# Gathered expert rows replaced by a dense sweep over all experts, once for each pair of token blocks

## The reference, cut to what matters

```python
def peer_ffn(h, w_q, sub_keys, u, v):          # u, v: (16384, 1024) a layer, 64 MB each
    def block(xb):                              # xb: 128 tokens x 1024
        q = (xb @ w_q).reshape(BLK, PEER_HEADS, PEER_QDIM)
        s1 = einsum('thd,hkd->thk', q[..., :64], sub_keys[:, 0])
        s2 = einsum('thd,hkd->thk', q[..., 64:], sub_keys[:, 1])
        v1, i1 = top_k(s1, 16); v2, i2 = top_k(s2, 16)
        cand = (v1[..., :, None] + v2[..., None, :]).reshape(BLK, 8, 256)
        sc, ci = top_k(cand, 16)
        e = i1[ci // 16] * 128 + i2[ci % 16]    # 8 heads x 16 = 128 experts a token
        g = softmax(sc)
        a = gelu(einsum('thkd,td->thk', u[e], xb)) * g
        return einsum('thk,thkd->td', a, v[e])
```

## Time and profile before

| | |
|---|---|
| runs | 2941.36 us median of 3 (2940.45 to 2948.73) |
| profiled execution, span from first to last instruction | 2939.0 us |
| PE, DVE, ACT, POOL busy | 78%, 74%, 40%, 44% |
| bytes read from HBM | 1164.28 MB, 398 GB/s with those written |

### The profile page before, as it was taken

How to read it: one execution, slowest core, us unless ns; L and a number is a source line. 1 busy time by engine, 2 the same in 40 slices (tenths; PEclk the granted TensorE clock), 3 DMA queues, 4 the chain that set the end, 5 groups by cost and what they waited for, 6 DMA issues and landing times.

```text
span 2939.0 us, 27902 instructions
## 1 busy us (share of the span) xinstructions
PE 2279.9 (78%) x7308; PEld 1206.3 (41%) x7308; DVE 2186.8 (74%) x5158; ACT 1182.4 (40%) x3443; POOL 1282.0 (44%) x1186
## 2 busy tenths in 40 slices
PE   8578787687887887787787878877788777886767
PEld 6535453354433544243443435433443434432222
DVE  2497768775878757796688877978779786887664
ACT  2144434343443433344444453435534454433333
POOL 0144334443355433454434544345434454355555
PEclk9789989999898998998899998989889898998889
DMA  6499999999999999999999999999999999999998
GB/s 253 150 401 421 404 362 422 420 421 389 413 410 421 421 393 412 421 411 421 414 382 402 421 421 416 392 403 417 421 406 392 405 421 421 391 411 422 422 422 359
DMA packets 170941, 1170.16 MB, mean 398 GB/s; under 512 B 19681, under 2 KB 19937, under 8 KB 36401
## 3 DMA queue, kind: packets, MB, share of 16 engines
q0 software_dynamic: 147456, 1073.81, 88.7%
q1 hardware_dynamic: 23344, 94.74, 8.2%
HBM read 1164.28 MB, written 4.19 MB: 398 GB/s over the span
## 4 chain that ended last, share of the span: by engine, by line
DMA 25%; DVE 15%; PE 12%; issue 6%; ACT 4%; POOL 3%; POOLq 0%; DVEq 0%; ACTq 0%; SPq 0%
DMA ring<-in_uv,pick_now 23%; PE acc L1650 7%; DVE ring L1076 5%; POOL ring L662 3%; PE ps L1448 3%; DVE side L1069 1%; DMA xc<-h 1%; ACT diag L1343 1%; DMA stream<-in_strips 1%; DVE arena L955 1%; ACT coef L1333 1%; DVE arena L936 1%; DVE arena L1026 1%; DVE arena L1030 1%; DVE arena L937 1%
## 5 line engine op out<-in xcount | busy, mean ns | idle before, releaser
L1650 PE MATMUL acc<-ring,diag 128*128 128x512 f32 x2988 | 1554.2, 663 | 487.9 <-ACT diag L1343 486.7
L662 POOL DMA_INDIRECT ring<-in_uv,pick_now x1024 | 1225.1, 1196 | 1514.3 <-PE acc L1650 1046.9
L1076 DVE CUSTOM_DVE_ANT_0 ring<-ring,h_now 128x1024 f32<-128x1024 f32 x1024 | 1237.3, 1223 | 518.5 <-DMA ring<-in_uv,pick_now 506.8
L1650 PEld LDWEIGHTS acc<-ring,diag 128*128 128x128 f32 x2988 | 586.3, 208 | 1316.9 <-ACT diag L1343 743.2
L1330 ACT ACTIVATE gelu<-dots 128x1 f32<-128x1 f32 x1024 | 206.1, 201 | 1253.9 <-DVE dots L1076 1252.4
L1069 DVE SCALAR_TENSOR_TENSOR side<-ring,coef,side 128x1024 f32<-128x1024 f32 x270 | 346.0, 1282 | 32.1 <-ACT coef L1333 32.0
L1343 ACT ACTIVATE diag<-ident,coef 128x128 f32<-128x128 f32 x747 | 300.0, 402 | 68.8 <-PE acc L1650 44.7
L1333 ACT ACTIVATE coef<-gate,gelu 128x1 f32<-128x1 f32 x1024 | 301.5, 294 | 33.2
L1448 PE MATMUL ps<-resident,actT 128*128 128x256 f32 x896 | 219.5, 402 | 0.0
L1448 PEld LDWEIGHTS ps<-resident,actT 128*128 128x128 f32 x896 | 177.1, 201 | 44.2 <-issue 19.6
L1435 PE MATMUL ps<-actT,stream 128*128 128x128 f32 x992 | 131.0, 294 | 28.5 <-DMA stream<-in_strips 24.3
(11 more groups left out here) (193 smaller groups left out, 1429.5 us busy)
## 6 DMA issues: line engine op xcount, KB each, us to landing
stream<-in_strips SPq DMA_DIRECT2D x104, 512.0 KB, 8.2
resident<-in_strips SPq DMA_DIRECT2D x18, 1024.0 KB, 12.4
ring<-in_uv,pick_now POOLq DMA_INDIRECT x1024, 12.5
ring<-in_strips SPq DMA_DIRECT2D x8, 1024.0 KB, 19.6
arena<-in_keys SPq DMA_DIRECT2D x8, 512.0 KB, 7.7
xc<-in_x SPq DMA_DIRECT2D x4, 512.0 KB, 6.9
h<-arena SPq DMA_DIRECT2D x4, 512.0 KB, 11.2
xc<-h SPq DMA_DIRECT2D x4, 512.0 KB, 7.8
```

The costliest lines, as they stand in the source:

```text
L662: pool.indirect_dma_start(ring[:, i, :], None, tables[layer], bass.IndirectOffsetOnAxis(ap=pick_now[:, half, i:i + 1], axis=0),).then_inc( ...
L1076: dve.tensor_tensor_reduce(ring[:, i, 0:D], ring[:, i, 0:D], h_now[:], 1.0, 0.0, ALU.mult, ALU.add, dots[:, i:i + 1]).then_inc(dotted, 1)
L1650: m = pe.matmul(acc[:, b * 512:(b + 1) * 512], diag[:, i % 4, :], ring[:, i, D + b * 512:D + (b + 1) * 512], start=(r == 0 and i == tensor ...
```

## The change

The eight stages become four passes of two blocks each: blocks (0, 1) and (2, 3) of layer 0, then of layer 1. A pass reads the whole `u` and the whole `v` of its layer, with plain DMAs from SP, and has three phases, counted in beats (`BEATS`):

- 128 beats "u": a tile of 128 experts is turned on DVE by two 32 x 32 block transposes (`turn_u`), and PE makes its dots with all tokens of the pass, eight products of 256 columns (`dot`). After every second tile ACT writes the gelu of them into `coef`, 128 tiles x 256 tokens (`gelu`).
- 64 beats "group" of four tokens: for each token DVE makes two matrices of 128 x 128 from `iota` (one-hot of one half of the expert's number; one-hot of the other half times the gate, `mark_lists`), PE multiplies them (`place`), which gives the token's gates over all 16384 experts, ACT copies the four out of the accumulator (`take_lists`), and POOL multiplies them into `coef`.
- 128 beats "v": a beat is 256 experts x 512 columns of `v`, and PE adds four products of 512 columns (`sum_up`), after a product with the identity that puts the residual ("seed") in.

Weight strips (none is kept now), `u`, seeds and `v` all go through one ring of four units of 512 KB. A new `AT` gives the beat before which each piece of the mixers and choices stands, for each block. In pass 0 the mixers of blocks 0 and 1 both stand before the first beat, their two choices beside the u phase; the mixer of block 2 begins at beat 128 and goes on beside the v phase, the mixer of block 3 has its last pieces at beats 318 to 320. In all passes nearly no piece stands between beats 132 and 192 of the pass. The gain of the second norm is now applied by ACT as a scale, and POOL copies the turned block to `hT2` (`keep`). The values of all tensors stay float32.

```diff
-SLOTS = 8
-RESIDENT = 9
+RING = 4
+TURNS = 3
+QUADS = 4
+TOKENS = 4
+PASSES = ((0, (0, 1)), (0, (2, 3)), (1, (0, 1)), (1, (2, 3)))
+def beats():
+    for n in range(len(PASSES)):
+        yield from (("u", n, i) for i in range(TILES))
+        yield from (("group", n, i) for i in range(groups_in(n)))
+        yield from (("v", n, i) for i in range(TILES))
...
@@ sync
+                elif u.what == "u":
+                    n, tile = u.key
+                    if tile % 2 == 0:
...
+                        for q in range(QUADS):
+                            sp.dma_start(
+                                ring[q * 32:(q + 1) * 32, at:at + 2, :].rearrange("p s (g c) -> p (s g) c", g=QUADS),
+                                tables[PASSES[n][0]][tile * P:(tile + 2) * P, q * STRIP:(q + 1) * STRIP].rearrange(
+                                    "(g j) c -> j g c", j=32),
+                            ).then_inc(loaded[at], 16)
@@ gpsimd
-                            pool.indirect_dma_start(
-                                ring[:, i, :], None, tables[layer],
-                                bass.IndirectOffsetOnAxis(ap=pick_now[:, half, i:i + 1], axis=0),
-                            ).then_inc(got[i], 16)
+                for group in range(groups_in(n)):
+                    at = groups_before(n) + group
+                    pool.wait_ge(built, at + 1)
+                    c = coef[:, :, group * TOKENS:(group + 1) * TOKENS]
+                    pool.tensor_tensor(c, c, lists[:, group % TURNS], ALU.mult).then_inc(scaled, 1)
@@ vector
-                        dve.tensor_tensor_reduce(ring[:, i, 0:D], ring[:, i, 0:D], h_now[:], 1.0, 0.0, ALU.mult,
-                                                 ALU.add, dots[:, i:i + 1]).then_inc(dotted, 1)
+            def mark_lists(n, group):
...
+                for i in range(TOKENS):
+                    t = group * TOKENS + i
+                    at = groups_before(n) * TOKENS + t
+                    if at >= TOKENS:
+                        dve.wait_ge(placed, at - TOKENS + 1)
+                    inner, outer = work[:, 2 * i * P:(2 * i + 1) * P], work[:, (2 * i + 1) * P:(2 * i + 2) * P]
+                    dve.tensor_scalar(inner, iota[:], listT[:, 2, t:t + 1], None, ALU.is_equal)
+                    dve.tensor_scalar(outer, iota[:], listT[:, 1, t:t + 1], listT[:, 0, t:t + 1], ALU.is_equal,
+                                      ALU.mult).then_inc(hot, 1)
+            def turn_u(n, tile):
...
+                for c in range(CUTS):
+                    m = 2 * (n * TILES + tile) + c
...
+                        dve.wait_ge((turn_used, dotted)[(m - TURNS) % 2], (m - TURNS) // 2 + 1)
+                    dve.transpose(turned_u[:, m % TURNS].rearrange("p k (g j) -> p g k j", g=QUADS),
+                                  u[:, :, c * CUT:(c + 1) * CUT, :]).then_inc(turned, 1)
@@ scalar
-                        act.activation(diag[:, i % 4, :], ident[:], ACT.Copy,
-                                       scale=coef[:, i:i + 1]).then_inc(diag_ready, 1)
+            def take_lists(n, group):
...
+                if group >= TURNS:
+                    act.wait_ge(scaled, at - TURNS + 1)
+                act.activation(lists[:, group % TURNS],
+                               acc[:, group % 2 * 512:(group % 2 + 1) * 512].rearrange("p (t i) -> p i t", t=TOKENS),
+                               ACT.Copy).then_inc(built, 1)
@@ tensor
-                            m = pe.matmul(acc[:, b * 512:(b + 1) * 512], diag[:, i % 4, :],
-                                          ring[:, i, D + b * 512:D + (b + 1) * 512],
-                                          start=(r == 0 and i == tensor[0][0]), stop=True, skip_group_check=True)
+            def dot(n, tile):
...
+                dst = acc[:, tile % 4 * 2 * P:(tile % 4 + 1) * 2 * P][:, tokens_of(n)]
+                for c in range(CUTS):
+                    m = 2 * at + c
+                    pe.wait_ge(turned, m + 1)
+                    for k in range(CUT):
+                        i = pe.matmul(dst, turned_u[:, m % TURNS, k, :], hT2[:, c * CUT + k, tokens_of(n)],
+                                      start=(c == 0 and k == 0), stop=(c == CUTS - 1 and k == CUT - 1))
+                    i.then_inc((turn_used, dotted)[c], 1)
+            def place(n, group):
...
+                if group >= 2:
+                    pe.wait_ge(built, at - 1)
+                for i in range(TOKENS):
+                    pe.wait_ge(hot, TOKENS * at + i + 1)
+                    pe.matmul(acc[:, (group % 2 * TOKENS + i) * P:(group % 2 * TOKENS + i + 1) * P],
+                              work[:, 2 * i * P:(2 * i + 1) * P], work[:, (2 * i + 1) * P:(2 * i + 2) * P],
+                              start=True, stop=True).then_inc(placed, 1)
+            def sum_up(n, v):
...
+                w = unit("v", n, v).rearrange("p (t c) -> p t c", t=2)
+                for t in range(2):
+                    for slot in range(2):
+                        i = pe.matmul(acc[:, slot * HALF_D:(slot + 1) * HALF_D],
+                                      coef[:, 2 * j + t, slot * P:(slot + 1) * P], w[:, t, :], start=False, stop=True,
+                                      skip_group_check=True)
+                i.then_inc(swept, 1)
```

More of the change, by code:

```diff
@@ L1 @@
 from contextlib import ExitStack
-from itertools import chain
 import numpy as np
@@ L69 @@
[L69 to L86, removed]
-    "gla": {
[13 rows of a table removed]
+CUT = KT // CUTS
+TILES = EXPERTS // P
+HALF_D = D // 2
+RING = 4
+TURNS = 3
+QUADS = 4
+TOKENS = 4
+SAYS = (
+    {1: "q", 3: "k", 7: "v", 11: "r", 15: "y", 16: "pq0", 17: "pq1", 18: "pq2", 19: "pq3"},
+    {3: "q", 4: "kv", 8: "y", 9: "pq0", 10: "pq1", 11: "pq2", 12: "pq3"},
+)
@@ new lines, in said, with chosen, preps_of, chain @@
+    def said(self, engine, event):
+        names = EVENTS[self.kind][engine]
+        base = BLOCKS * len(EVENTS["gla"][engine]) if self.layer else 0
+        return self.p * len(names) + base + names.index(event) + 1
+    def chosen(self, engine, event):
+        names = CHOSEN[engine]
+        return self.turn * len(names) + names.index(event) + 1
+def preps_of(n):
+    return [Prep(n, slot) for slot in range(len(PASSES[n][1]))]
+def chain():
+    for n in range(len(PASSES)):
+        preps = preps_of(n)
+        if n == 0:
+            yield from ((prep.kind, prep) for prep in preps)
+            yield from (("pick", prep) for prep in preps)
+        else:
+            for prep in preps:
+                yield prep.kind, prep
+                yield "pick", prep
@@ new lines, with blocks_in, groups_in, groups_before @@
+CHAIN = list(chain())
+def blocks_in(n):
+    return len(PASSES[n][1])
+def groups_in(n):
+    return blocks_in(n) * P // TOKENS
+def groups_before(n):
+    return sum(groups_in(m) for m in range(n))
+def sweep(n):
+    if blocks_in(n) == 2:
+        return [(h, j) for h in range(2) for j in range(TILES // 2)]
+    return [(h, j) for j in range(TILES // 2) for h in range(2)]
+def begins(n, v):
+    return v % (TILES // 2 if blocks_in(n) == 2 else TILES) == 0
+def phases_before(n):
+    return sum(blocks_in(m) for m in range(n))
@@ new lines, in stores_before, with beats_in, order @@
+def stores_before(n):
+    return sum((4 if blocks_in(m) == 2 else 1) for m in range(n))
+def beats_in(n):
+    return groups_in(n) + 2 * TILES
+def beats():
+    for n in range(len(PASSES)):
+        yield from (("u", n, i) for i in range(TILES))
+        yield from (("group", n, i) for i in range(groups_in(n)))
+        yield from (("v", n, i) for i in range(TILES))
+BEATS = list(beats())
+def order(engine):
+    return sorted((beat, i, piece) for i, (kind, prep) in enumerate(CHAIN)
+                  for piece, beat in zip(PIECES[kind][engine], AT[i][engine]))
@@ L239, in __call__, with beside @@
         self.settle()
+def beside(engine, pieces, dense):
+    at = [next(p) for p in pieces]
+    done = 0
+    for beat, i, piece in order(engine):
+        while done < int(beat):
+            dense(*BEATS[done])
+            done += 1
+        assert at[i] == piece, (engine, at[i], piece)
+        at[i] = next(pieces[i], None)
+    for beat in BEATS[done:]:
+        dense(*beat)
 def build(nc, x, positions, gain_mix, gain_ffn, strips0, strips1, w_lr, w_alpha, b_alpha, gla_gain,
@@ new lines, in choose @@
+                for half in range(2):
+                    each = onehot[:, half, 0:H * TOPK * TOPK].rearrange("p (h k j) -> p h k j", h=H, j=TOPK)
+                    step.mark(dve.tensor_tensor(
+                        each, each, both(topf)[:, half, hs].rearrange("p h (o j) -> p h o j", o=1).to_broadcast(
+                            [P, H, TOPK, TOPK]), ALU.mult))
+                step.settle()
+                dve.tensor_reduce(ef[:, :, hs].rearrange("p a h k -> p a (h k)"), hits, AX, ALU.add)\
+                   .then_inc(chosen["dve"], 1)
@@ new lines, in dense @@
+            def dense(what, n, beat):
+                if what == "u":
```

(20 more changed lines are left out.)

1526 lines of the change are left out of this document (733 added, 793 removed), and 55 rows, old and new, of tables (AT, LATE, PIECES, STRIPS_OF).

## The result

The changed kernel takes 5125.22 us (median of 4 runs, 5123.13 to 5129.81); the kernel before took 2942.43 (2940.45 to 2948.73, 4 runs beside it). The ratio is 1.7425, 95% interval 1.7399 to 1.7451: much slower, as forecast (5200), and 75 us under the forecast.

What follows compares the result with a forecast made beforehand. Bytes (DMA) were taken to bound the kernel before, DVE and PE each at three quarters. Terms 1782 + 1771 + 540 + 210 + 768 + 57 + 60 + 8 = 5196 us, forecast 5200, range 4800 to 5650.

Steps and rivals of the forecast that it cites:

- A: PE's dots in the u phases: 4096 products of 256 columns at 0.435 us, 1782 us.
- B: PE's sums in the v phases: 2048 products of 512 columns and 16 seeds at 0.858 us, 1771 us.
- C: PE's other work outside the opening, taken from its earlier busy time: 540 us.
- D: Opening: mixers 0 and 1 one after the other ahead of the first dot, 210 us with POOL's copy.
- E: Group phases: 256 groups, DVE's 2.0 us and POOL's 1.0 one after the other, 768 us.
- F + G + H: In order: seams between phases 57 us, PE's pieces with late DVE or ACT partners 60, the last store 8.
- Rival 3: PE's pieces wait (5390 us), or its clock is 0.91 throughout, dots and sums rising by 351 (5550); chance 0.14.
- Rival 1: Group phases: DVE and POOL run beside each other, POOL's 1.0 us hidden behind 2.0, time 4944 us; chance 0.2.
- rival 2: Group phases: POOL's product or the tokens' chain is slow, 4.2 us a group, time 5500 us; chance 0.12.
- The load, put at nothing: u phase: loading 1 MB takes 3.5 us and hides behind PE's 7.0, with two pairs in the ring.
- Rival 4: The u load sets the pace, deciding from about 10 us a MB; at 12.4, +1380 us, time 6580; chance 0.07.
- Rival 5: Whole kernel: not slower, the halved bytes decide at 1.7 ms because PE's dense products cost less; chance 0.01.

Runs made afterwards that it cites:

- consts_first: The changed kernel with POOL making its constants before, not after, it issues its 16 small loads: 5124.31 us.
- pool_quarter: The changed kernel with three quarters of POOL's multiplication in the group phases left out: 4911.14 us.
- dve_mul: The changed kernel with the group's product moved from POOL to DVE, which reads the gates straight from the accumulator: 4993.23 us.
- half_k: The changed kernel with half of each dot's products left out, all loads kept: 4740.35 us.
- half_k_spread: As half_k, but each DMA of u writes a quarter of the columns to all 128 partitions instead of all columns to 32: 4586.3 us.
- quarter: The changed kernel with three of four chunk products of each half dot and three quarters of each sum's columns left out: 3958.23 us.

## Why the prediction came out right, step by step

| term | forecast | measured | from |
|---|---|---|---|
| A dots | 1782 | 1794 | L1667 |
| B sums and seeds | 1771 | 1797 | L1702 1774.5 + seeds 22.6 |
| C other PE work | 540 | 497 | 4791.9 less all the others |
| D opening | 210 | 231 | window |
| E group phases | 768 | 759 | 199.8 + 186.3 + 186.3 + 186.2 |
| F + G + H idle of PE | 125 | 64 | idle of the u, v and seam windows |
| sum | 5196 | 5141, less 18 in both C and E | |

The last row: 18 us of PE's other work ran inside group windows, so the span is 5123. The terms missed by +12, +26, -43, +21, -9 and -61 us: part of the closeness of the sum is that these cancel.

**The unit prices held.** 0.435 us for a 256-column product read off 32 products before became 0.436 over 1024; together A and B missed by 1%. This is why a forecast of 5200 for a kernel that did not exist came within 1.5%: 68% of it was count times cadence, from stretches where PE ran back to back with a new weight each time. The mean ns of a record (663 in the earlier trace rows) would have been the wrong price: 2 x 663 for 512 columns gives 2.7 ms for the sums.

**C was too high by 43** because the same products are shorter now. The 1344 records of 256 columns with strips took 333.0 us before (219.5, 87.0 and 26.5 in the trace's three groups) and take 311.5; those of 128 columns 136.2 before, 122.3 now. That is 35 of the 43 us. The granted clock in the u and v phases, where PE has no gaps, is 0.99 to 1.00; it was 0.91 over serving. Rival 3's second half, 0.91 throughout, fell by the same rows.

**D was too low by 21.** It splits by PE's timeline. The first product came 9.4 us late, at 18.9 instead of 9.5: I had left the new order of the loads out. Between the first mixer's last copy (121.73) and the second's first product (128.72) lie 7.0 us, and my 9.5 less 3 had left 6.5 for it. This step held, though PE idles 9.2 us there, since ACT asks for the second block's `x` only behind the first block's eight scaled copies, and it lands 3.7 us later (timeline of ACT):

```profile
119.56 2.17 ACT L1167 ACTIVATE actT<-ps,gffn 128x128 f32<-128x128 f32 x8 [3.89 <-PE ps L1407]
121.50 0.33 ACTq L1188 DMA_DIRECT2D arena<-in_x  x1
125.20 1.06 ACT L1193 ACTIVATE actT<-arena 128x1024 f32<-128x1024 f32 x1 [3.47 <-DMA arena<-in_x]
```

The rest, some 11 us, is in the two mixers themselves: from first product to turned block they took 102.9 and 100.7 us, where 106 less 9.5 had left 96.5. About 5 of it is the step "without the gain spread's 3.8". Before, these products ran from 80.79 to 84.56 us, but ACT's copies beside them, which the next products need as well, ended only at 83.08 (timeline of before):

```profile
80.90 2.18 ACT L1155 ACTIVATE actT<-ps,ggla 128x128 f32<-128x128 f32 x8 [4.84 <-PE ps L1396]
84.50 15.74 PE L1448 MATMUL ps<-ring,actT 128*128 128x256 f32 x64
```

So taking the gain spread away frees 1.4 us a mixer, not 3.8. PE's waits for strips, which I had put at nothing, are 3 us; the last 3 stay open.

Of the late start, consts_first shows that the order on POOL's queue alone is not the cause: of 9.4 us it gave 2.4 back at the first product and 1.0 at the first dot. The other thing that changed is when the first `x` is asked for. Before, it was SP's first load, asked for at 0.84 us, and ACT used it at 4.87; now ACT asks for it at 3.88, behind SP's first strips, and uses it at 14.22 (11.74 in consts_first). That this order is what delays it was not tried.

**E was right in mechanism, and in size partly by luck.** One after the other, not beside: the 1.42 us mask over the 1.25 us product, pool_quarter and dve_mul each show it. DVE's part was 1.65 for seven masks in place of 2.0, POOL's 1.25 in place of 1.0: two errors of opposite sign. Three of the four phases took 186.2 or 186.3 us, where 192 was forecast; the first took 13.5 more, with products of block 2's mixer in it. Rival 1 (4944) and rival 2 (5500) both fell. The Trainium skill, SBUF — State Buffer, section "SBUF: two separate sides", has DVE in a two-port mode and GpSimd exclude each other for whole instructions; these durations agree with it. The estimate from the Trainium skill, GPSIMD Engine Reference, section "Performance versus the Vector engine", was 1.1 us for POOL's product, against 1.25 measured.

**G was too high.** I allowed 60 us for late partners and 57 for seams; all gaps in u, v and seam windows are 64. F's 15 us for the last choice of pass 0 was idle time on top of C; of the 18.3 us of that seam PE idled only 2.4. Nearly all the rest was the first products of block 2's mixer (13.0 us of line 1426), which C counts already. PE's pieces seldom found their partner late.

**The load, put at nothing, was the least certain step, and here the trace says wrong where the time did not.** "DMA share well under a half" was wrong in the u phases: 0.68 to 0.71. The packet arithmetic from two queues gave 3.5 us for a pair; at full share it is 4.8 by the last u window (1.05 MB at 152 / 0.69 = 220 GB/s), and half_k took 5.3 with the share at 0.93. The price of a packet was not the fault: sent to all 128 partitions, half_k_spread's pair at full share is 3.3 us (1.05 MB at 226 / 0.71 = 318 GB/s). The step that failed is that I priced the load to 32 partitions like any other, after naming the rule that spoke against it. Rival 4's threshold, about 10 us a pair, was also too far off: lateness cost 23 us with the mean well under PE's 7.0. The sign and size of the result never hung on it.

**Rival 5** (half the bytes decide) is refuted most plainly by quarter: with a quarter of PE's columns the dense form still takes 3958.

## What to carry to other kernels

When bytes bind and PE stands at 78%, halving the bytes by multiplying PE's columns by 2.7 only changes the bound, as here: multiply columns by the back-to-back cadence first, and stop if that alone exceeds the old time. Next, look for what stands behind it, as quarter did; here loads, group phases and opening together were above the old time too. And where two engines hold each other up, try giving both parts to the faster one: here it won 132 us.

## What was not expected of the hardware

- Loads of 1 KB pieces to 32 neighbouring partitions: landing 5.0 us against 3.7 to all 128, 1.48 times the DMA engines' time per byte (half_k and half_k_spread, same bytes and packets). Why it is this much stays open.
- The granted clock stood at 0.51 through group phases with PE busy 74% of the time (137.0 of 186.2 us), and at 0.99 to 1.00 in the u and v phases around them. Each group is eight records in 2.2 us and then 0.7 us without any. In pool_quarter, with eight records in 1.8 us and 0.2 us without any, it stood at 1.00. The low clock cost nothing here that the traces show, since DVE bound the phase.
- A DVE mask held up by POOL lasted at most 1466 ns against a median of 335, and it is the mask that is stretched even where it starts first (800.77 against POOL's 800.86). Which instruction is hit shows in the maximum of a line, not in its median.
- A DVE product of 512 columns straight from the accumulator takes 674 ns, the same as one from SBUF (686); ACT's copy of 0.60 us ahead of POOL was needed only for POOL.
